# First block's layer norms: affine part folded into the modulation columns, stream scaled later, head reordered

## The reference

```python
for i in range(DEPTH):                      # DEPTH = 2
    mod = silu(c) @ ada_w[i] + ada_b[i]     # six rows: sh1, sc1, g1, sh2, sc2, g2 (and the same for c_ctx)
    h = x * (1.0 + sc1) + sh1
    y = retention_mixer(h, ...) if i == 0 else neighbourhood_mixer(h, ...)
    x = layer_norm(DN_ALPHA * x + g1 * y, ln_g[i, 0], ln_b[i, 0])
    h = x * (1.0 + sc2) + sh2
    x = layer_norm(DN_ALPHA * x + g2 * sq_relu_mlp(h, mlp_w1[i], mlp_w2[i]), ln_g[i, 1], ln_b[i, 1])
    ...                                     # the same for ctx, where i == 0
```

## Time and profile before

| | us |
|---|---|
| median of 3 runs | 2769.17 |
| the profiled execution, its own time | 2769.07 |
| its span in the trace | 2767.4 |
| PE busy | 2669.4 |
| DVE busy | 1849.1 |
| ACT busy | 602.0 |
| POOL busy | 119.9 |

### The profile page before, as it was taken

How to read it: one execution, slowest core, us unless ns; L and a number is a source line. 1 busy time by engine, 2 the same in 40 slices (tenths; PEclk the granted TensorE clock), 3 DMA queues, 4 the chain that set the end, 5 groups by cost and what they waited for, 6 DMA issues and landing times.

```text
span 2767.4 us, 32244 instructions
## 1 busy us (share of the span) xinstructions
PE 2669.4 (96%) x13451; PEld 2144.4 (77%) x13451; DVE 1849.1 (67%) x2028; ACT 602.0 (22%) x1270; POOL 119.9 (4%) x90
## 2 busy tenths in 40 slices
PE   5999999899999899899899999999999999999999
PEld 3777676677877685699788888788878888877887
DVE  3456464754445648788876778787677677777766
ACT  2111111211211117421210233521020013342111
POOL 0000000100000002110000001010000000100000
PEclk8999999999999999999999999999999999999999
DMA  6422323343344355266455544355556545444653
GB/s 255 140 101 97 137 76 122 118 153 128 130 142 165 120 148 100 68 209 196 157 186 171 178 162 151 124 168 190 176 164 200 179 164 169 148 150 139 197 169 129
DMA packets 251520, 420.33 MB, mean 152 GB/s; under 512 B 35104, under 2 KB 92832, under 8 KB 251376
## 3 DMA queue, kind: packets, MB, share of 16 engines
q1 hardware_dynamic: 247968, 410.09, 45.1%
q0 software_dynamic: 2272, 5.07, 0.6%
q10 hardware_dynamic: 1136, 3.12, 0.3%
HBM read 417.19 MB, written 1.05 MB: 151 GB/s over the span
## 4 chain that ended last, share of the span: by engine, by line
PE 89%; DVE 6%; ACT 2%; issue 2%; DMA 1%; POOL 1%; ACTq 0%; DVEq 0%
PE psum L429 86%; PE psum L443 3%; DVE wgt_lo L1485 1%; POOL small L2135 1%; DMA raw<-ada_w 1%; ACT xh L1003 0%; DVE wgt_hi L1483 0%; DVE psum L1727 0%; PE psum L657 0%; ACT n_prob_b L1003 0%; DVE xl L1506 0%; ACT L1003 0%; ACT W L1003 0%; DVE n_probT L1738 0%; DVE xl L1494 0%
## 5 line engine op out<-in xcount | busy, mean ns | idle before, releaser
L1485 DVE TENSOR_TENSOR wgt_lo<-raw,wgt_hi 128x2048 fp32r<-128x2048 f32 (+2 forms) x344 | 771.7, 2243 | 11.8
L429 PE MATMUL psum<-wgt_hi,xh 128*128 128x512 f32 (+2 forms) x1840 | 710.5, 386 | 2.8 <-DVE xl L1506 1.2
L429 PE MATMUL psum<-wgt_hi,xl 128*128 128x512 f32 (+2 forms) x1840 | 700.9, 381 | 0.0
L429 PE MATMUL psum<-wgt_lo,xh 128*128 128x512 f32 (+2 forms) x1840 | 700.4, 381 | 0.0
L1483 DVE CAST wgt_hi<-raw 128x2048 fp32r<-128x2048 f32 (+2 forms) x344 | 411.8, 1197 | 311.5 <-PE psum L429 130.5
L429 PEld LDWEIGHTS psum<-wgt_hi,xh 128*128 128x128 f32 x1840 | 349.2, 190 | 78.7 <-issue 12.0
L429 PEld LDWEIGHTS psum<-wgt_hi,xl 128*128 128x128 f32 x1840 | 348.9, 190 | 66.6
L429 PEld LDWEIGHTS psum<-wgt_lo,xh 128*128 128x128 f32 x1840 | 349.1, 190 | 64.4 <-issue 1.0
L429 PE MATMUL psum<-wgt_hi,yh 128*128 128x512 f32 x928 | 366.1, 395 | 2.5 <-DVE yl L1494 1.1
L429 PE MATMUL psum<-wgt_hi,yl 128*128 128x512 f32 x928 | 361.9, 390 | 0.0
L429 PE MATMUL psum<-wgt_lo,yh 128*128 128x512 f32 x928 | 361.8, 390 | 0.0
(11 more groups left out here) (188 smaller groups left out, 2104.2 us busy)
## 6 DMA issues: line engine op xcount, KB each, us to landing
raw<-mlp_w SPq DMA_DIRECT2D x64, 1024.0 KB, 5.3
raw<-w_in SPq DMA_DIRECT2D x60, 1024.0 KB, 5.0
raw<-ada_w SPq DMA_DIRECT2D x48, 1024.0 KB, 7.2
raw<-ffn_w_gate SPq DMA_DIRECT2D x40, 1024.0 KB, 5.2
raw<-ffn_w_up SPq DMA_DIRECT2D x40, 1024.0 KB, 5.1
raw<-ffn_w_down SPq DMA_DIRECT2D x40, 1024.0 KB, 5.1
raw<-ret_w_in SPq DMA_DIRECT2D x24, 1024.0 KB, 5.3
raw<-nat_w_in SPq DMA_DIRECT2D x12, 1024.0 KB, 5.3
```

Source lines behind the costliest of these rows:

```text
L429: return pe.matmul(o, l, r, start=start_, stop=stop, skip_group_check=True)
L1485: v.tensor_tensor(wgt_lo[:, s % RING, :size], r, wgt_hi[:, s % RING, :size], ALU.subtract).then_inc(split_done.sem, split_done.up())
```

## The change

- **Norm.** `add_and_norm` does `(x - mean) * rstd` in one `tensor_scalar` per tile (`normalise`), for tile `tt - 1` after tile `tt`'s epsilon. `ln_g` and `ln_b` are no longer applied there.
- **Fold.** Their columns (`lnc`, loaded in the head, transposed once) go into the modulation columns: `fold` makes `sh + sc * ln_b` and `sc * ln_g`. For the second block's first norm the same is done with `first_gain` and `first_bias`.
- **Scale.** `X` itself gets its affine part and the factor ALPHA later, in `scale_row`, two `scalar_tensor_tensor` of 128x1024 per tile. After edges 1 and 3 it stands in the up part of the mlp's first chunk, one tile after each `low`. After edge 2 both tiles stand right behind `low_x2("h1")`. After edge 4 both stand right behind `low_pairs("f1")`, with factor 1, and ACT's squares wait for them (`x_final`).
- **Turning.** `turn_normed` transposes each tile as soon as it is ready, all units open at once (8 banks for 4 tiles, 4 for 2), instead of waiting for all tiles. The first two weight tiles take each feature tile in turn (`arriving`).
- **Gates.** Layer 0's second gate has its own buffer, so ACT writes it without waiting for the last retention tile's use of the first.
- **Ahead.** Between the two column halves of an mlp's last chunk (`between`), DVE splits three blocks ahead, and does the modulation columns that stood at the end; PE's modulation blocks and transposes of parts 3 and 4 move earlier.
- **Two tiles.** In `h1m` and `f1` ACT and DVE share the affine step (`operand_pairs`, `low_pairs`).
- **Head.** The transposes of `X` stand between the modulation blocks; rq's weight block is asked for ahead of the last of them (`ask_block`); the decay table's DMA is issued later.

```diff
 def features_by_tokens(...):
+    for kt, j in [(kt, j) for kt in range(KT) for j in range(2)] if arriving else [(kt, j) for j in range(2) for kt in range(KT)]:
+        if arriving and j == 0:
+            pe.wait_ge(out_of(ready(kt)), emptied(ready(kt)))
...
+def turn_normed(name, tiles):
+    per = 4 // tiles
+    for tt in range(tiles):
+        pe.wait_ge(x_ready.sem, x_ready.next())
+        for u in range(KT // per):
+            o = open_unit(pe, (name, u), "dve") if tt == 0 else bank_of((name, u))
+            for j in range(per):
+                at = (j * tiles + tt) * P
+                ins = pe.transpose(o[:, at:at + P], X[:, tt, (per * u + j) * P:(per * u + j + 1) * P], ident)
+            if tt == tiles - 1:
+                close_unit((name, u), ins)
+    return lambda kt: (name, kt // per)
...
 # PE, head
-for n in range(4):
+for n in range(3):
     modulation(0, 0, n)
 pe.wait_ge(x_in.sem, x_in.at(32))
-ready = features_of("h0", X, range(4), range(4))
+ready = features_of("h0", X, range(4), range(2))
+modulation(0, 0, 3)
+modulation(0, 1, 0)
+features_of("h0", X, range(4), range(2, 3))
+modulation(0, 1, 1)
 modulation_columns(0, 0)
-for n in range(4):
-    modulation(0, 1, n)
-features_of("h0", X, range(4), range(4, 5))
+features_of("h0", X, range(4), range(3, 4))
+modulation(0, 1, 2)
+features_of("h0", X, range(4), range(4, 5), {4: unit(("ada", 0, 0))["bank"]})
+ask_block(wb(0, KT, 0, 2 * P))
+modulation(0, 1, 3)
 modulation_columns(0, 1)
...
 # PE, mlp
+more_up = {2: {0: 0, 2: 1}, 3: {0: 2, 2: 3}}.get(c, {}) if layer == 0 else {}
+def in_last_down(b):
+    if layer == 0 and b in (0, 2):
+        modulation_columns(1, 4 if b == 0 else 3)
+    if layer == 1 and b == 0:
+        vectors(0)
...
 # DVE
-def keep_up(key, ahead=2):
+def keep_up(key, ahead=2, beyond=0):
...
-        if b["index"] >= u["taken"] + RING:
+        if b["index"] >= u["taken"] + RING + beyond:
...
+def low_pairs(name, cols):
+    dve.wait_ge(mod_folded.sem, mod_folded.now())
+    for u in range(KT // 2):
+        if u % 2 == 0:
+            affine_pair(name, u + 1, cols)
+        low((name, u), xl[:, 2 * u:2 * u + 2, 0:T], xh[:, 2 * u:2 * u + 2, 0:T], 1)
...
+def fold(layer, part):
+    v.tensor_tensor(t, sc, bias, ALU.mult)...
+    v.tensor_tensor(sh, sh, t, ALU.add)
+    v.tensor_tensor(sc, sc, gain, ALU.mult).then_inc(mod_folded.sem, mod_folded.up())
...
+def scale_row(tt, factor, then=x_scaled, table=ln_gb):
+    x = X[:, tt, :]
+    if tt == 0:
+        dve.wait_ge(ln_in.sem, ln_in.next(2))
+    v.scalar_tensor_tensor(out=x, in0=x, scalar=factor, in1=table[:, 0, :], op0=ALU.mult, op1=ALU.mult)...
+    v.scalar_tensor_tensor(out=x, in0=table[:, 1, :], scalar=factor, in1=x, op0=ALU.mult, op1=ALU.add)...
...
 # DVE, add_and_norm
+    def normalise(tt):
+        x, mv = X[:, tt, :], small[:, 80 + 2 * tt:82 + 2 * tt]
+        dve.wait_ge(rstd_dve.sem, rstd_dve.next())
+        v.tensor_scalar(x, x, mv[:, 0:1], small[:, 92 + tt:93 + tt], ALU.subtract, ALU.mult).then_inc(x_ready.sem, x_ready.up())
     for c in range(2):
+        if c and between:
+            between()
...
-            v.scalar_tensor_tensor(out=x, in0=x, scalar=mv[:, 0:1], in1=ln_gb[:, 0, :], op0=ALU.subtract, op1=ALU.mult)...
-            v.scalar_tensor_tensor(out=x, in0=x, scalar=small[:, 92 + tt:93 + tt], in1=ln_gb[:, 1, :], op0=ALU.mult, op1=ALU.add)...
+            if tt != tts[0]:
+                normalise(tt - 1)
+    normalise(tts[-1])
...
 # DVE, mlp
         low((("up", layer), c * KT + kt), ...)
+        if c == 0 and kt in tts:
+            scale_row(kt, ALPHA)
...
+    def between():
+        keep_up((("down", layer, c), 0, tts[-1]), 3, 1)
+        if layer == 0:
+            modulation(1, 4)
+            modulation(1, 3)
+            fold(1, 3)
...
 # DVE, after the mlp of layer 0
 low_x2("h1", 1, 0)
-prescale(range(2))
+for tt in range(2):
+    scale_row(tt, ALPHA, table=ln_gb2)
 ...
 keep_up(("nq", KT - 1))
...
 # DVE, second block, first layer
-    gained("f1", V_FFN1, (0, 1))
+    low_pairs("f1", first_columns)
+    for tt in range(TT):
+        scale_row(tt, 1.0, x_final)
 ...
 mean_square()
 feed_forward(1, 4 * i + 1)
...
 # ACT, second block, first layer
+    operand_pairs("f1", first_columns, 4)
+    act.wait_ge(x_final.sem, x_final.at(2))
 ...
     ins = squares_of(c, None)
```

More of the change, by code:

```diff
@@ L272, in take_block @@
             split_blocks.append({"block": block, "release": None})
+            asked.append(s)
+        def take_block(pe, source):
+            if not asked:
+                ask_block(source)
+            s = asked.pop(0)
+            block = split_blocks[s]["block"]
+            assert block["shape"] == source.shape
             view = lambda t: t[:, s % RING, :block["size"]].rearrange("p (a b) -> p a b", a=block["shape"][1])
@@ L538, in features_of, with vectors @@
                     transposes((name, u), "dve", [src[:, tt, kt * P:(kt + 1) * P]
-                                                  for kt in range(per * u, per * u + per) for tt in tts])
+                                                  for kt in range(per * u, per * u + per) for tt in tts],
+                               banks[u] if banks else None)
+                return lambda kt: (name, kt // per)
+            def vectors(i):
+                now["layer"] = i + 1
+                pe.wait_ge(lay_in.sem, lay_in.at(16 * N_LAYER_DMAS * (i + 1)))
+                transposes(("lvec",), "act", [l_rows[0:V_ROWS, :]])
+            def turn_normed(name, tiles):
[9 more added lines that the diff above has]
+                            close_unit((name, u), ins)
                 return lambda kt: (name, kt // per)
@@ L702, in _ @@
             gates(1, 5, 1)
-            pe.wait_ge(x_ready.sem, x_ready.next(2))
-            ready = features_of("h1m", X, range(2))
-            mlp(1, range(2), ready)
+            mlp(1, range(2), turn_normed("h1m", 2))
             def turn_x(name, us, source=None, after=None):
@@ L1037, in mod_row, with operand_pairs @@
-            def mod_row(layer, part):
+                                [((s * T, (s + 1) * T), *columns_of(layer, part)(kt, s)) for s in range(2)])
+            def operand_pairs(name, cols, folded):
+                act.wait_ge(mod_folded.sem, mod_folded.at(folded))
+                for u in range(KT // 2):
+                    dst = xh[:, 2 * u:2 * u + 2, 0:T]
+                    if u % 2:
+                        act.wait_ge(affine_done.sem, affine_done.next())
+                        operand((name, u), dst)
+                    else:
+                        operand((name, u), dst, [((j * T, (j + 1) * T), *cols(2 * u + j)) for j in range(2)])
@@ L1039, in mod_row @@
+            def mod_row(layer, part, last=None):
                 act.wait_ge(psum_full.sem, filled(("ada", layer, part)))
-                before = ("mod", *divmod(6 * layer + part - 1, 6))
+                before = ("mod", layer, last) if last else ("mod", *divmod(6 * layer + part - 1, 6))
                 if (now["layer"], before) in units:
@@ L1671, in _ @@
                     ins.then_inc(dve_out.sem, dve_out.up())
+                if h == 0:
+                    keep_up(("ln",))
+                    dve.wait_ge(psum_full.sem, filled(("ln",)))
+                    v.tensor_copy(lnc[:, :], bank_of(("ln",))[:, 0:64]).then_inc(dve_out.sem, dve_out.up())
+                    dve.wait_ge(dve_out.sem, dve_out.now())
                 modulation(0, 2 + h)
+                if h == 2:
+                    fold(0, 3)
                 st, mv = small[:, 32:56], small[:, 80:88]
@@ L1776, in _ @@
             add_and_norm(range(2), lambda c, tt: ("ny", c, tt), ("gate", 1, 2, 0, 1))
-            low_x("h1m", range(2))
-            prescale(range(2))
-            v.memset(small[:, 323:324], 0.0).then_inc(tab_free.sem, tab_free.up())
-            mlp(1, range(2))
+            low_pairs("h1m", columns_of(1, 3))
             v.memset(yh_pad.bitcast(F32), 0.0)
```

229 lines of the change are left out of this document (127 added, 102 removed).

## The result

The kernel after takes 2751.87 us, the median of 4 runs (2747.88 to 2757.64), against 2768.23 for the kernel before beside it: ratio 0.9941, 95% interval 0.9929 to 0.9953. That is 16.4 us between medians; 2750 was predicted, with a range of 2740 to 2759.

A forecast was written before the change was run, and what follows sets the result against it. PE was taken as the bound, busy 2669.4 of 2767.4 us, leaving some 98 us idle to win. Terms 8.0 + 10.7 + 5.2 + 1.4 - 6.2 = 19.1 off 2769.07 gave 2750 us, range 2740 to 2759.

The forecast's parts named there:

- head: Kernel's start up to rq: last modulation block 1.4 us earlier, rq's block already split; gain 8.0 us.
- edge 1: Norm and turning of X behind retention: X ready at 509.05 instead of 516.5; gain 10.7 us.
- edge 2: Norm ahead of nk: PE restarts earlier, then waits 4.3 us for a split behind two rows; gain 5.2 us.
- edge 3: Attention's layer norm, two tiles: X ready at 1160.0, first split behind the first affine step; gain 1.4 us.
- edge 4: Norm ahead of the first feed-forward: PE starts 4.5 us earlier, then waits 9 us for a split; loss 6.2 us.
- Norm step: DVE's new normalise per tile, one `tensor_scalar` on 128x1024 with two column operands: taken at 0.80 us.
- single-rate rival: The normalise step takes 1.28 us instead of 0.80, all four edges come later: 2754 us, chance 0.13.
- "late block" rival: In the head, the last modulation block comes 2.6 us later instead of 1.4 earlier: 2754 us, chance 0.13.
- two new waits: PE waits for a split queued behind scale rows: 4.3 us at nk, 9 us in the first feed-forward.
- No new waits: Splits come in time behind the edges: 37 us gained with the head, 2732 us, chance 0.08.
- Everything lands on the path: Ten rows, the squares and four clock restarts use up the 37 us gained: 2769 us, chance 0.06.
- the clock: PE held at 1.2 GHz some 10 us after each of six stops, 5 us each: slower, 2777 us, chance 0.04.

The follow-up runs named there:

- h_noask: Kernel after with rq's weight block loaded behind the last modulation block instead of asked for ahead of it: 2754.73 us, ratio 0.9942 to the kernel before.
- e_edge4: Kernel after with splits put before and between the two scale rows of the first feed-forward, a third right behind: 2742.63 us, ratio 0.9912 to the kernel before.
- e_edge2: Kernel after with the split of the second nk block put in front of that edge's two scale rows: 2750.62 us, ratio 0.9939 to the kernel before.
- e_mod: Kernel after with DVE's part 4 modulation columns moved ahead of the four adds in the first mlp's last chunk: 2744.59 us, ratio 0.9917 to the kernel before.
- e_all: Kernel after with the edits of e_mod, e_edge2 and e_edge4 together: 2730.43 us, ratio 0.9867 to the kernel before.
- e_all3: e_all plus the mlp's first weight block split between the column halves at the attention's layer norm: 2726.94 us, ratio 0.9842 to the kernel before.

## Why the prediction was right, and where it was not

The lead over the kernel before was followed through both traces; the places where it changes give the terms:

| term | predicted | in the traces |
|---|---|---|
| head | +8.0 | +7.0 |
| edge 1 | +10.7 | +10.0 |
| last chunks of the first mlp | none | -7.5 |
| edge 2 | +5.2 | +6.2 |
| attention | none | -3.3 |
| edge 3 | +1.4 | +3.2 |
| edge 4 | -6.2 | -5.6 |
| second layer change | none | +1.4 |
| sum | 19.1 | 11.4 |

In the third row after's lead is counted without 2.4 us of PE's own work (a modulation block and two groups of transposes), which after has done by then and before does at edge 2.

- **Norm step.** Right: 0.807 us for the 0.80 taken. The single-rate rival falls. The rule of the Trainium skill ("VectorE: DVE Perf Modes", section "Mode 2×_2P — use both read ports for one tensor") thus agrees with these rows for two column operands too, at 0.12 us above the row with a constant (0.68).
- **Head.** The mechanism held (rq's block split ahead, at the price of an `xl` behind rk's split). The last modulation block came 0.3 us earlier, not 1.4: h_noask shows that the megabyte put ahead of it costs 2.2 us. So it came between the forecast and the "late block" rival, which had it 2.6 us later than before.
- **Edge 1.** Right within 0.7 us. X was ready 0.9 us sooner than reckoned, 0.6 of it because POOL's answer came 1.17 us after the epsilon's end and not 1.75. The prediction carried the 1.75 over as a constant; the rows show that it held the step that the change removes (POOL's 1.52 us beside DVE's 1.28, 1.05 beside 0.80), so a shorter norm step is won twice. But the stretch behind the restart ran at 0.57 for 4 us, 1.7 us, for which this step had nothing.
- **Edges 2 and 4.** The two new waits came where they were placed: 3.74 and 8.38 us, for 4.3 and 9. e_edge4 confirms the cause as it stands; e_edge2's is seen in the trace and only supported by the times.
- **Edge 3.** Wrong in size, 3.2 for 1.4 us: the 4.83 us wait behind the first affine step was foreseen, one for the fourth block was not met, and X was again ready sooner (7.3 us after the first tile's start, not 7.9).
- **The step that failed** is in edge 2's: "only the 0.75 us wait is saved", that is, the modulation blocks and columns that move ahead of the last matmul were costed at nothing. PE's own time for them is the same wherever they stand. But a moved transpose opens a PSUM bank, and who frees it moved too: to behind three splits and four adds on DVE. 6.2 us of wait and 1.3 of clock behind it. The working named what was queued behind the rows at edges 2 and 4, and did not do so for `between`. e_mod shows this cause.
- **The total.** 2750 against 2751.87 is thus partly luck. The five terms that were forecast sum to 20.8 for 19.1, and the three that were not (-7.5, -3.3 and +1.4) bring the profiled execution to 11.4; the median comes near 2750 because it lies 6 us below that execution.
- **The other rivals.** "No new waits" gave 2732 for a kernel in which the splits come in time; e_all is nearly that kernel (no wait for `mod` either, but still 4.83 us for a split at edge 3), and takes 2730.43. "Everything lands on the path" (2769) and "the clock" (2777) are out by the time measured.

## What to carry to other kernels

When work is taken out of a wait and put behind it, write down the engine's program from there on and look for the first thing another engine needs: here three splits, moved to stand before, between and right behind two rows, were worth 9.2 us at one edge, and all four reorderings made 16 us into 41. Do the same for the consumer of each thing that is moved earlier: a tiny block (0.24 us on DVE) that holds a PSUM bank stopped PE for 6.2 us. And where two engines keep pace, the slower one's whole chain per tile counts: 0.73 us more per tile cost 7.3 us in twelve tiles. Look also at what runs beside a short step on the critical path: POOL's answer came 0.6 us sooner when DVE's pass beside it became 0.5 us shorter, and a DVE cast of 0.29 us took up to 3.19 beside a POOL addition.

## What the runs showed of the hardware

- DVE and POOL hold each other up in some pairs of steps here. POOL's 128x1 step on SBUF took 0.57 us while DVE worked on PSUM, 1.05 beside a 0.80 us `tensor_scalar` over X, 1.41 beside two such passes (0.68 and 0.81) and 1.52 beside a 1.28 us `scalar_tensor_tensor`. A DVE cast from SBUF to SBUF (0.29 us) took 0.75 to 3.19 us where it met POOL's 3.45 us addition, and ended 0.15 or 0.16 us after it in all 14 traces, while DVE's steps on PSUM beside another of these additions kept their 0.68 and 0.69 us.
- A stop of PE does not cost a fixed amount of clock. The same 2.18 us wait at edge 2 was followed by 8 us at full clock in after and e_edge2, and by 0.79 in e_edge4; a stop of about 3 us in the attention by 4 us at 0.64 in one execution and by 8 us at 0.50 and 4 at 0.59 in another. The Trainium skill ("TensorE: Matmul & The Clock Gate", section "Part 1: The HAM clock gate (the "warmup" mystery)") says that the point at which the clock changes differs from run to run for one kernel; these rows agree.
- For a change of some 10 us in this kernel, one profiled execution is therefore no measure of the total. Its rows up to a given step are: the gate matmuls at edge 1 start within 1.4 us of each other in ten kernels with the same head.
- The kernels with fewer stops have the higher mean granted clock: 0.984 before, 0.986 after, 0.991 in e_all3's profiled executions. Part of what a removed wait gives can come that way: in the trace e_edge4 took out 7.8 us of wait, and in the 8 us behind it, which ran at 1.00 for 0.69, another 2.2.
